# RWKV and retention state products in smaller parts, throwaway TensorE products at two places, and another order on GpSimd

## What is computed

```python
for l in range(DEPTH):
    f = swiglu(h, w_gate[l, 0], w_up[l, 0], w_down[l, 0])
    h = layer_norm(ALPHA * h + 0.5 * f, ...)
    if l % 2 == 0:
        m, s_sh, s_rw, s_rt = ab_mixer(h, pos, st_shift[i], st_rwkv[i], st_ret[i], p, i)
    else:
        m, s_cv, s_gd = gdn_mixer(h, st_conv[i], st_gdn[i], p, i)
    h = layer_norm(ALPHA * h + m, ...)
    f = swiglu(h, w_gate[l, 1], w_up[l, 1], w_down[l, 1])
    h = layer_norm(ALPHA * h + 0.5 * f, ...)

# RWKV-7, one token:    S = S*w - (S kk)(kk*a)^T + v k^T ;  o = S r
# retention, one chunk: o = (q S)*xi + inner ;  S = g*S + kz^T v
# gated delta, one token: S = a (I - beta k k^T) S + beta k v^T ;  o = S^T q
```

## Time and profile before

| | us |
|---|---|
| median of 3 runs | 1494.38 |
| lowest, highest | 1490.0, 1495.59 |
| profiled execution | 1494.03 |
| its span | 1492.2 |
| mean granted TensorE clock, as a share of full speed | 0.977 |
| TensorE busy | 1408.7 (94%) |
| VectorE, ScalarE, GpSimd busy | 904.9, 647.6, 444.1 |

### The profile page before, as it was taken

How to read it: one execution, slowest core, us unless ns; L and a number is a source line. 1 busy time by engine, 2 the same in 40 slices (tenths; PEclk the granted TensorE clock), 3 DMA queues, 4 the chain that set the end, 5 groups by cost and what they waited for, 6 DMA issues and landing times.

```text
span 1492.2 us, 30453 instructions
## 1 busy us (share of the span) xinstructions
PE 1408.7 (94%) x12008; PEld 1333.6 (89%) x12008; DVE 904.9 (61%) x1213; ACT 647.6 (43%) x983; POOL 444.1 (30%) x455
## 2 busy tenths in 40 slices
PE   7999999887999899999999999999997889999996
PEld 7999998876868589999999999988987769999996
DVE  4444447976464365555567775567787566655554
ACT  4333336524224253343454433376683445334333
POOL 3333031631323021115211116430006741111343
PEclk9999999999889799999999999999999989999998
DMA  7555543301242154555445555423434015555541
GB/s 281 168 168 175 172 140 96 114 17 32 90 152 81 43 183 157 167 160 184 151 129 168 157 171 175 151 92 124 142 108 157 31 71 170 157 167 158 190 156 51
DMA packets 50621, 203.37 MB, mean 136 GB/s; under 512 B 5696, under 2 KB 5696, under 8 KB 49760
## 3 DMA queue, kind: packets, MB, share of 16 engines
q1 hardware_dynamic: 46224, 181.03, 38.0%
q0 software_dynamic: 4016, 19.81, 3.7%
q10 hardware_dynamic: 288, 1.18, 0.2%
HBM read 192.17 MB, written 9.83 MB: 135 GB/s over the span
## 4 chain that ended last, share of the span: by engine, by line
PE 81%; DVE 9%; ACT 5%; issue 3%; POOL 1%; DMA 0%; ACTq 0%; POOLq 0%; DVEq 0%
PE gemm L2601 23%; PE gemm L2605 22%; PE gemm L2602 22%; DVE wlo L2538 2%; ACT whi L2533 2%; PE gemm L2628 1%; PE job L858 1%; PE job L1741 1%; DVE M L2106 1%; PE job L1680 0%; PE job L2610 0%; POOL xsum L3134 0%; PE job L876 0%; PE job L728 0%; DVE M L2279 0%
## 5 line engine op out<-in xcount | busy, mean ns | idle before, releaser
L2601 PE MATMUL gemm<-xhi,whi 128*128 128x290 f32 (+1 forms) x2032 | 619.5, 305 | 27.3 <-DVE wlo L2538 19.8
L2533 ACT ACTIVATE whi<-raw 128x1024 fp32r<-128x1024 f32 (+1 forms) x319 | 358.3, 1123 | 619.3 <-PE gemm L2605 616.0
L2538 DVE TENSOR_TENSOR wlo<-raw,whi 128x1024 fp32r<-128x1024 f32 (+1 forms) x319 | 434.6, 1363 | 312.3 <-ACT whi L2533 309.8
L2605 PE MATMUL gemm<-xlo,whi 128*128 128x290 f32 (+1 forms) x2032 | 609.3, 300 | 0.7 <-DVE xlo L402 0.7
L2602 PE MATMUL gemm<-xhi,wlo 128*128 128x290 f32 (+1 forms) x2032 | 606.9, 299 | 0.0
L2601 PEld LDWEIGHTS gemm<-xhi,whi 128*128 128x128 f32 x2032 | 388.9, 191 | 45.5 <-DVE wlo L2538 23.7
L2602 PEld LDWEIGHTS gemm<-xhi,wlo 128*128 128x128 f32 x2032 | 389.6, 192 | 1.8
L2605 PEld LDWEIGHTS gemm<-xlo,whi 128*128 128x128 f32 x2032 | 388.6, 191 | 2.3 <-DVE xlo L402 1.4
L2601 PE MATMUL gemm<-hhi,whi 128*128 128x288 f32 x704 | 209.6, 298 | 2.5 <-POOL hlo L3150 1.8
L2602 PE MATMUL gemm<-hhi,wlo 128*128 128x288 f32 x704 | 209.9, 298 | 0.0
L2605 PE MATMUL gemm<-hlo,whi 128*128 128x288 f32 x704 | 209.2, 297 | 0.0
(11 more groups left out here) (445 smaller groups left out, 1475.4 us busy)
## 6 DMA issues: line engine op xcount, KB each, us to landing
raw<-in_w_dram SPq DMA_DIRECT2D x255, 512.0 KB, 3.5
raw<-in_w_dram SPq DMA_DIRECT2D x64, 704.0 KB, 4.1
M<-in_ret_in_dram POOLq DMA_DIRECT2D x1, 2048.0 KB, 9.7
out_ret_s_dram<-M POOLq DMA_DIRECT2D x1, 2048.0 KB, 8.1
s_space<-in_gdn_in_dram POOLq DMA_DIRECT2D x4, 512.0 KB, 5.1
M<-in_gdn_in_dram POOLq DMA_DIRECT2D x4, 512.0 KB, 5.5
out_gdn_s_dram<-s_space POOLq DMA_DIRECT2D x4, 512.0 KB, 4.2
out_gdn_s_dram<-M POOLq DMA_DIRECT2D x4, 512.0 KB, 6.1
```

Of the source, the lines that this page charges most:

```text
L2533: nc.scalar.activation(whi[c % SPL][:, 0:w], raw[c % RAW][:, 0:w], ACT.Copy).then_inc(hi_ready, 1)
L2538: nc.vector.tensor_tensor(wlo[c % SPL][:, 0:w], raw[c % RAW][:, 0:w], whi[c % SPL][:, 0:w].bitcast(F32), ALU.subtract).then_inc(lo_ready, 1)
L2601: pe.matmul(bank[:, 0:w_], whi[s][:, w], hi[:, f0 + q, 0:w_], start=first, stop=False)
L2605: mm = pe.matmul(bank[:, 0:w_], whi[s][:, w], lo[:, f0 + q, 0:w_], start=False, stop=last)
```

## The change

- The old-state products are in two halves, `old_products((0, 1))` behind `sgram` and `old_products((2, 3))` behind `sY`, in pieces 3 and 4; the job list puts `sP` ahead of `sMV`.
- The new-state products are in four parts, `new_states(0)` to `new_states(3)`, at the head of four successive pieces, with VectorE's `into_state(t)` likewise. The rotations and head sums are shared out among these pieces; `gnv` follows rotations 5 to 7 in one piece.
- `rQ` 0 and 1 stand behind `rS` in the piece after unit 14, `rQ` 2 ahead of `rO` 2 after unit 15, `rQ` 3 behind the stage. VectorE's `qx` and ScalarE's `state_part` follow.
- GpSimd does all eight cosines before it waits for `sS`; so the store of RWKV's state and the load of retention's are issued behind them, after the fourth part.
- `keep_busy(14, 2, "abo")` stands behind the last sum, ahead of `abo`'s second halves.
- In the delta rule, three throwaway products stand before `updates(0)` and seven between it and `updates(1)`; the waits on `round_free` are set apart for them.
- On GpSimd in the delta rule, `sample_inputs()` is called at level 2, behind that level's masks and ahead of the wait for `q_t0`.

```diff
@@ -513,8 +511,8 @@
-            def keep_busy(n, j=0):
-                wait_count(pe, bank_free[j], TABLE["zb"][3][j])
+            def keep_busy(n, j=0, name="zb"):
+                wait_count(pe, bank_free[j], TABLE[name][3][j])
                 for _ in range(n):
...
@@ -569,6 +567,33 @@
                 fin(pe.matmul(bank[:, 0:T], C("rot"), b_z[:, t, :], start=True, stop=True), ("rot", t))
+
+            pbanks = []
+
+            def old_products(ts):
+                for t in ts:
+                    for b in range(DB):
+                        o, at = (t * DB + b) * 8, SEQ + DS * b
+                        mms = [pe.matmul(pbanks[e][half(e), o:o + 8], a_s0[half(e), t, b, :],
+                                         kr[half(e), t, :, at:at + DS], start=True, stop=True) for e in range(2)]
+                    if t == 3:
+                        for e in range(2):
+                            fin(mms[e], ("sP", e))
+
+            def new_states(t):
+                bank = start(("sS", t))
+                if t % 2:
+                    pe.wait_ge(sem("s_ub_high"), (t + 1) // 2)
+                for e in range(2):
+                    h = 2 * t + e
+                    pe.matmul(bank[half(e), 0:512], a_nat[NROW, 2, 1, h * 64:(h + 1) * 64], s_vb[:, h, :, :],
+                              start=True, stop=False)
+                for e in range(2):
+                    h = 2 * t + e
+                    rhs = s_ub_low[:, h, :, :] if h < 6 else s_ub_high[:, h - 6, :, :]
+                    mm = pe.matmul(bank[half(e), 0:512], a_nat[NROW, 2, 2, h * 64:(h + 1) * 64], rhs,
+                                   start=False, stop=True)
+                fin(mm, ("sS", t))
...
@@ -706,6 +731,9 @@
                     fin(mms[e], ("sgram", e))
+                pbanks.extend(start(("sP", e)) for e in range(2))
+                pe.wait_ge(sem("rwkv_in"), 16)
+                old_products((0, 1))
                 yield
...
@@ -720,15 +748,7 @@
                 fin(mm, ("sY", 0))
-                banks = [start(("sP", e)) for e in range(2)]
-                pe.wait_ge(sem("rwkv_in"), 16)
-                for t in range(4):
-                    for b in range(DB):
-                        o, at = (t * DB + b) * 8, SEQ + DS * b
-                        mms = [pe.matmul(banks[e][half(e), o:o + 8], a_s0[half(e), t, b, :],
-                                         kr[half(e), t, :, at:at + DS], start=True, stop=True) for e in range(2)]
-                for e in range(2):
-                    fin(mms[e], ("sP", e))
+                old_products((2, 3))
                 yield
...
@@ -762,56 +782,40 @@
                 yield
+                pe.wait_ge(sem("s_masked"), 1)
+                pe.wait_ge(sem("s_ub_low"), DB)
+                new_states(0)
                 rotate(2)
                 rotate(3)
-                rotate(4)
-                pe.wait_ge(sem("s_masked"), 1)
-                pe.wait_ge(sem("s_ub_low"), DB)
-                for t in range(4):
-                    bank = start(("sS", t))
-                    if t % 2:
-                        pe.wait_ge(sem("s_ub_high"), (t + 1) // 2)
-                    for e in range(2):
-                        h = 2 * t + e
-                        pe.matmul(bank[half(e), 0:512], a_nat[NROW, 2, 1, h * 64:(h + 1) * 64], s_vb[:, h, :, :],
-                                  start=True, stop=False)
-                    for e in range(2):
-                        h = 2 * t + e
-                        rhs = s_ub_low[:, h, :, :] if h < 6 else s_ub_high[:, h - 6, :, :]
-                        mm = pe.matmul(bank[half(e), 0:512], a_nat[NROW, 2, 2, h * 64:(h + 1) * 64], rhs,
-                                       start=False, stop=True)
-                    fin(mm, ("sS", t))
-                yield
+                yield
+                new_states(1)
                 for k in (("OS", 1, 0), ("OS", 1, 1), ("sO", 0)):
...
                 head_sums("gnm", a_ld)
+                rotate(4)
+                yield
+                new_states(2)
                 rotate(5)
...
                 rotate(7)
-                yield
                 pe.wait_ge(sem("gn_sq"), 1)
...
                 yield
+                new_states(3)
                 pe.wait_ge(sem("rotated"), 8)
...
                 by_token("rkn", 4, 2)
-                pe.wait_ge(sem("qx"), 1)
-                pe.wait_ge(sem("ret_in"), 16)
-                from_state(0)
                 yield
...
                 by_token("rvn", 8, 1)
-                from_state(1)
                 by_token("rvn", 8, 2)
...
                 scores(0)
-                from_state(2)
                 scores(1)
-                from_state(3)
                 scores(2)
...
@@ -822,6 +826,10 @@
                     fin(mm, ("rS", j))
+                pe.wait_ge(sem("qx"), 1)
+                pe.wait_ge(sem("ret_in"), 16)
+                from_state(0)
+                from_state(1)
                 pe.wait_ge(*out(("ratt", 1)))
...
@@ -830,6 +838,7 @@
                 ret_sum("rgm", 0)
+                from_state(2)
                 ret_out(2)
...
@@ -838,6 +847,7 @@
             stage("zb", 1, lambda k: next(piece))
+            from_state(3)
             ret_out(3)
...
@@ -846,6 +856,7 @@
             ret_sum("rgv", 3)
+            keep_busy(14, 2, "abo")
...
@@ -1036,22 +1047,21 @@
                 yield
-                act.wait_ge(sem("stored"), 48)
-                state_part(0)
                 values(0)
                 values(1)
-                state_part(1)
                 values(2)
                 yield
-                state_part(2)
-                state_part(3)
+                act.wait_ge(sem("stored"), 48)
                 yield
...
                 copy(key, b_s[:, 0, :, :], jb(key).rearrange("p (h v) -> p h v", h=4))
+                state_part(0)
+                state_part(1)
                 ret_copy(0)
...
                 yield
+                state_part(2)
                 ret_square(0)
...
@@ -1333,18 +1346,14 @@
                                                 op0=ALU.mult, op1=ALU.add), key)
+                rotated(4)
+                yield
+                into_state(2)
                 rotated(5)
...
                 yield
-                dve.wait_ge(sem("stored"), 48)
-                dve.wait_ge(sem("rotated"), 8)
-                for q in range(2):
-                    V.tensor_tensor(b_qx[:, :, tok(q)], b_z[:, 0:4, tok(q)],
-                                    C("xi").rearrange("p (h t) -> p h t", h=4), ALU.mult)
-                V.tensor_tensor(b_qx[:, :, SEQ:T], b_z[:, 0:4, SEQ:T],
-                                C("xi4").rearrange("p (h t) -> p h t", h=4), ALU.mult).then_inc(sem("qx"), 1)
-                yield
+                into_state(3)
                 key_rows(0)
...
@@ -1360,6 +1369,13 @@
                 yield
+                dve.wait_ge(sem("stored"), 48)
+                dve.wait_ge(sem("rotated"), 8)
+                for q in range(2):
+                    V.tensor_tensor(b_qx[:, :, tok(q)], b_z[:, 0:4, tok(q)],
+                                    C("xi").rearrange("p (h t) -> p h t", h=4), ALU.mult)
+                V.tensor_tensor(b_qx[:, :, SEQ:T], b_z[:, 0:4, SEQ:T],
+                                C("xi4").rearrange("p (h t) -> p h t", h=4), ALU.mult).then_inc(sem("qx"), 1)
                 decayed(0)
...
@@ -1505,12 +1521,11 @@
-            cosines(0, 5)
+            cosines(0, 8)
             for t in range(4):
...
             pool.dma_start(b_s0, a["ret_in"]).then_inc(sem("ret_in"), 16)
-            cosines(5, 8)
             pool.wait_ge(sem("gn_done"), 4)
...
@@ -1854,13 +1869,20 @@
                         small("dsO", 1, q_aq, q_u, ("dsU", 1))
+            def keep_busy(n):
+                for _ in range(n):
+                    pe.matmul(gemm[3][:, 0:SEQ], C("mean"), xsum[:, 0:SEQ], start=True, stop=True)
+
             head_norms(4)
             head_norms(3)
+            pe.wait_ge(sem("round_free1"), 4)
+            keep_busy(3)
             updates(0)
+            keep_busy(7)
             updates(1)
...
                 pe.wait_ge(sem(f"o_free{e}"), 4)
-                pe.wait_ge(sem(f"round_free{e}"), 4)
+            pe.wait_ge(sem("round_free0"), 4)
             stage("gdo", 6)
...
@@ -2427,10 +2449,10 @@
                     masked_decays()
-                    sample_inputs()
                 else:
...
                     if l == 2:
+                        sample_inputs()
                         pool.wait_ge(sem("q_t0"), 1)
...
                         for ck in range(4):
```

More of the change, by code:

```diff
@@ L184, in plan_jobs @@
     jobs.extend(("OS", q, e) for q in range(2) for e in range(2))
-    jobs.extend([("sgram", 0), ("sgram", 1), ("sMV", 0), ("sY", 0), ("sP", 0), ("sP", 1), ("sXT", 0), ("sX", 0),
-                 ("sU", 0), ("sO", 0)])
-    jobs.extend(("rot", t) for t in range(5))
-    jobs.extend(("sS", t) for t in range(4))
```

(28 more changed lines are left out.)

## The result

| | before | changed |
|---|---|---|
| median, us | 1494.38 (5 runs, 1490.0 to 1499.01) | 1477.98 (5 runs, 1473.34 to 1481.07) |
| profiled execution | 1494.03 (span 1492.2) | 1473.34 (span 1471.5) |
| mean granted clock, profiled execution | 0.977 | 0.991 |

The ratio is 0.9892, 95% interval 0.9866 to 0.9918: 16 us less, 12 to 20. The forecast was 1471.5, range 1464 to 1482: the median lies in the range, 6.5 over the forecast. The sum was made from the profiled execution of the kernel before; that of the changed kernel lies 1.8 over the forecast.

A forecast was written before the change was run, and what follows sets the result against it. TensorE, 81% of the chain, was taken to bound the kernel, with time won only where it is slow or idle. Terms of 4.75, 4.9, 2.2, 8.5, 3.6 and 2.0 made 25.95, less 3.4 reserve: 22.55, so 1471.5 us, range 1464 to 1482.

The forecast's parts named there:

- A: Old-state products in zb, in two halves: full clock there and in the unit behind, one wait gone; 4.75 us less.
- B: New-state products in zb, in four parts with units between: full clock kept, a VectorE wait gone; 4.9 us less.
- retention: Retention's products from old state: two of four leave the stage's pieces for its tail; net 2.2 us less, bounds 0 to 3.4.
- C: Ahead of abo: fourteen throwaway products hide in 5.90 us of idle and keep abo at full clock; 8.5 us less.
- D: Delta rule, level 2: GpSimd's masks before the sample inputs; product 2.0 us sooner, rest at full clock; 3.6 us less.
- E: Delta rule's state updates: throwaway products in idle time speed the second update and next unit; 2.0 us less, bounds 0.6 to 3.5.
- first rival: In zb: thin products still lose the clock even when split; 1478.7 us (1475 to 1483), chance 0.22.
- the reserve: 3.4 us held back for new clock falls between the old-state halves and at retention's pair from old state.
- late-load rival: Retention's state load, issued later, makes TensorE wait and takes gains back; 1484 to 1493 us, chance 0.09.
- The new wait of the variance sums: In zb, variance sums sharing a piece with three rotations wait for VectorE to empty their banks; put at 1.2 us.
- The slower rival: Ahead of abo and in the delta rule: throwaway products start at half clock and cost double; 1502.6 us, chance 0.05.
- the prediction's bound of 2.0: Delta rule, level 2: only 2.0 us won if the remaining idle of 3.6 us still takes the clock.

The follow-up runs named there:

- retention's groups apart: Changed kernel with retention's first old-state product group ahead of its new state, the second behind, three throwaway products between; 0.9875 to before, median 1475.38.
- level 2 filled: Changed kernel with six throwaway products in TensorE's idle time between the halves of level 2's product in the delta rule; 0.9874 to before, median 1473.96.
- old-state products mixed: Kernel before with four throwaway products in the middle of its 128 old-state products; 1.0016 to before, 2.4 us slower.
- both additions: Changed kernel with retention's groups apart, three throwaway products between, and six throwaway products in level 2's idle time; 0.9880 to before, median 1476.7.

## Why the prediction came out as it did

The table gives stretches of TensorE's timeline from the start of one weight unit to that of another (units counted from 0): zb's unit 3 to 6 (A), zb's unit 6 to abo's second halves (B and retention), those to abo's unit 3 (C), zg's last unit but one to gdo (D, and E's updates and delay), gdo's first two units (E's clock). "Old" are profiles in which the stretch's code is that of before, "new" those with the change; the two kernels with retention's groups apart are left out of the second row, and runs with one of D and E alone, or level 2 filled, out of the fourth.

| stretch | old | mean | new | mean | less | forecast |
|---|---|---|---|---|---|---|
| A | 25.11 to 25.14 (4) | 25.13 | 19.94 to 19.95 (7), 21.43, 24.48 | 20.61 | 4.5 | 4.75 |
| B, retention | 90.93 to 95.58 (7) | 93.53 | 85.11 to 86.62 (5) | 86.30 | 7.2 | 4.9 + 2.2 |
| C | 14.81, 18.08, 18.28, 18.53, 22.11, 22.53 | 19.06 | 14.01 to 14.03 (7) | 14.02 | 5.0 | 8.5 |
| D, E's updates | 96.06 to 97.35 (5) | 96.94 | 93.46 to 95.50 (5) | 94.68 | 2.3 | 3.6 + 0.95 - 0.3 |
| E's clock | 8.68 to 9.73 (6) | 8.91 | 7.48 to 7.86 (8) | 7.79 | 1.1 | 1.4 |

**A** was right in its steps (2.03 and 2.04 for a forecast of about 2.1, and 5.2 less in seven of nine profiles). In the other two the clock falls at a half, 3.7 and 0.7 less. That is the first rival, in some executions and not in others; the prediction had it as all or nothing.

**B and retention** are right in sum: 7.2 by profiles, 7 to 8.5 by taking them out. The new-state products lose the clock for 10.24 to 13.65 in all seven profiles that have them in one piece and in none of the seven that have them in parts. Part of the sum is luck: the forecast was read from an execution with 90.95 there, against which 86.60 is 4.4 less. Five of the seven old profiles lose the clock in zb's last units too, which the forecast didn't count. Inside the sum the clock does fall at the pair, as the reserve supposed, in all five profiles that have the pair side by side; moved apart, the stretch from unit 6 is 1.8 shorter (84.84 against 86.60). The load of retention's state lands 11.8 after its issue at 440.68, not 9.7: at 452.5, 1.8 ahead of the pair at 454.28 instead of 4. The late-load rival was nearer than I had it, and didn't come. The new wait of the variance sums, put at 1.2, is 0.4 in the changed kernel (0.19 and 0.22, at 431 and 432).

**C** is the term that was mis-sized most: 8.5 forecast, 4.0 measured alone (2.1 to 6.0), 5.0 by profiles. The mechanism was right to the row: products at 1.98, no idle left, full clock. Wrong was the step that abo runs at 0.50 "up to 515.51", 20.2 us: one execution's stretch, taken as the price. In the other five profiles with abo's code unchanged the stretch takes 14.81 to 22.53. The throwaway products make it 14.02 each time, so their worth is the difference to the mean, not to the execution that I read. The slower rival (products already at half clock) didn't come here, but four products in the run with old-state products mixed show its mechanism.

**D** is right in what ends last: the mask was the wait, VectorE's read is the next one. The 2.0 were to be had. What the clock adds differs: with the order alone, in the second profile of the changed kernel and with the groups apart the stretch takes 93.38 to 93.54, although level 2 is at half clock for 3.41 in each. That is 3.4 to 3.6 under the old mean, about the forecast's 3.6, and 2.5 to 2.7 under the 96.06 of the execution that the sum was made from. In the other three profiles with the new order it takes 95.40 to 95.50; two of them are at half clock for 6.83 in level 2 and lose 0.75 to a fall ahead of it, the third for 6.83 further on, at 1171. With level 2 filled nothing is lost there. So the idle that is left takes the clock in most executions, as the prediction's bound of 2.0 supposed. VectorE's 3.08 fell to 0.42 with loads still in flight at a DMA share of 0.99, so the loads weren't its cause. The Trainium skill (SBUF — State Buffer, "SBUF: two separate sides") has such a VectorE operation and a GpSimd operation lock each other out; the trace agrees in the length, 3.08 beside the masks and 0.42 without them. It also says that the one that starts first goes on; that isn't seen here, since VectorE's row starts at 1144.87 and the masks' at 1145.17.

**E** is right in the update (1.14) and nearly in the units behind (1.1 for 1.4). Wrong is the step that put the delay at 0.3 and counted the update's 0.95 as won: six rows take 1.46 and fourteen 3.29, and gdo then starts when ScalarE's xhi is there, not at the update's end. From L1715 to gdo that is 0.2 lost (8.93 for 8.76), not 0.65 won; E is worth 0.9 in all, where 2.0 were forecast.

**The rule on idle gaps.** The Trainium skill (TensorE: Matmul & The Clock Gate, "Why this matters for your kernels") asks for no idle gaps between bursts; the runs at abo agree (5.90 and 3.75 of idle, clock lost; filled, clock kept). Idle is not the whole cause: no idle row stands in the 8 us ahead of the falls at the new-state products (422.75) and at retention's pair (457.72 in the changed kernel). The old-state halves don't decide it, since they also remove a wait of 0.66 ahead of the fall.

**The sum.** The means of the table make 20.1 less, the forecast was 22.55 less, measured are 16 and 18. Before its reserve of 3.4 the forecast was 25.95: 3.5 too much in C, 2.25 in D and E, the rest right; so the reserve paid for errors that it wasn't made for. Against the one execution that the sum was made from, the changed kernel's first profile is 5.2 less in A, 4.4 in B and retention, 8.1 in C, 0.6 in D with the updates and 2.2 in E's clock, 20.5 together. There C is as forecast, and what is missing lies in B and retention and in D: that this profile came within 1.8 of the forecast is errors that cancel. Between the table and the times some 3 stay open. One thing points to the choice of execution: the profiled execution was the fastest of its kernel's in both runs of the changed kernel, with new-state parts and halves alone, without new-state parts, with level 2 filled and with both additions; in before it lay near the median. But with GpSimd's order alone it was the slowest, and with the groups apart among the slowest, so this is a hint and no more. Which falls the executions without a trace had isn't seen. Single results (4.0, 4.3, 1.8, 4.9 and some 7.5) make 22.5, with 1 to 3 to either side on the first four and some 5 on the last; that parts share a gain is neither shown nor excluded.

## What to carry to other kernels

Read what the clock costs from several executions, not from one: a borderline stretch falls in some and not in others, and an edit that removes it is worth its mean. Cover an idle time whole or leave it: fourteen products held the clock in all seven profiles that have them, and five, with 3.75 of idle left, lost it as before in the one profile taken. Put throwaway products ahead of the fall: in the one profile with some behind it they cost double and didn't bring the clock back at once.

## What the runs showed of the hardware

In six profiles of kernels whose code in abo is that of before, the same work took 14.81 to 22.53, with 6.81 to 23.87 at half clock. A busy TensorE doesn't keep the clock by itself: it fell at the four new-state products with no idle time in the 8 us before, in seven profiles of seven, and with a weight unit of 3.4 between the parts in none of seven. And a product at half clock takes twice its time, but the clock didn't come back for 3.78 of throwaway products in a row (393.81 to 397.52, still 0.50 until 406.53).
